# The first four panels of the output projection, each one head output earlier

## The reference, cut to what matters

```python
gla_o = merge_heads(rms_norm(gla_o, gla_norm_w[layer]))        # 4 heads of 256
hgrn_o = merge_heads(rms_norm(hgrn_o, hgrn_norm_w[layer]))     # 4 heads of 128
xo = merge_heads(rms_norm(xo, xattn_norm_w[layer]))            # 4 heads of 128
mixed = jnp.concatenate([gla_o, hgrn_o, xo], axis=-1).astype(dtype)
mixed = mixed * jax.nn.silu(gate)                              # 256 x 2048
x = x + jnp.einsum('bse,ed->bsd', mixed, w_out[layer]).astype(dtype)   # w_out 2048 x 1024
```

## Time and profile before

| what | us |
|---|---|
| median of 3 runs (lowest, highest) | 1028.63 (1028.36, 1029.28) |
| the profiled execution, its own time | 1030.11 |
| span of the profiled execution, first to last instruction | 1028.3 |
| TensorE busy | 1004.7 |
| VectorE, ScalarE, GpSimd busy | 534.0, 486.5, 765.5 |

### The profile page before, as it was taken

How to read it: one execution, slowest core, us unless ns; L and a number is a source line. 1 busy time by engine, 2 the same in 40 slices (tenths; PEclk the granted TensorE clock), 3 DMA queues, 4 the chain that set the end, 5 groups by cost and what they waited for, 6 DMA issues and landing times.

```text
span 1028.3 us, 21621 instructions
## 1 busy us (share of the span) xinstructions
PE 1004.7 (98%) x8212; PEld 984.2 (96%) x8212; DVE 534.0 (52%) x898; ACT 486.5 (47%) x748; POOL 765.5 (74%) x602
## 2 busy tenths in 40 slices
PE   9999999999999999999999899999999989999996
PEld 7999999999999999999899899999999989999996
DVE  5925984457544444504755463466656464444203
ACT  6543324456654444444566534433255554444441
POOL 2896666657999888996586845577539929999993
PEclk9999999999999999999999899999999999999998
DMA  9563334343565555555462213433226726665561
GB/s 319 163 203 127 123 105 143 119 128 107 181 198 183 175 171 174 165 174 181 126 186 91 72 54 114 142 125 122 85 65 199 215 95 195 195 196 184 173 185 58
DMA packets 48330, 154.62 MB, mean 150 GB/s; under 512 B 6060, under 2 KB 11188, under 8 KB 48264
## 3 DMA queue, kind: packets, MB, share of 16 engines
q1 hardware_dynamic: 46112, 151.31, 47.3%
q10 hardware_dynamic: 2152, 2.38, 0.7%
HBM read 151.57 MB, written 2.10 MB: 149 GB/s over the span
## 4 chain that ended last, share of the span: by engine, by line
PE 88%; DVE 4%; ACT 3%; POOL 2%; issue 1%; DMA 1%; SPq 0%; DVEq 0%; ACTq 0%
PE panel L1659 69%; PE panel L1709 3%; PE aux L1812 2%; POOL wlo L622 2%; PE panel L1759 1%; DMA memk<-in_mem_panels 1%; PE aux L2058 1%; PE aux L2069 1%; PE panel L1745 1%; PE aux L2032 1%; DVE tmp L1080 1%; PE aux L2098 1%; PE aux L2107 1%; PE aux L2021 1%; PE aux L1929 1%
## 5 line engine op out<-in xcount | busy, mean ns | idle before, releaser
L622 POOL TENSOR_TENSOR wlo<-raw,whi 128x512 fp32r<-128x512 f32 x554 | 736.4, 1358 | 239.7 <-ACT whi L722 221.3
L1659 PE MATMUL panel<-xh,whi 128*128 128x256 f32 (+1 forms) x1440 | 417.9, 290 | 4.7 <-DVE xl L1069 4.1
L1659 PE MATMUL panel<-xh,wlo 128*128 128x256 f32 (+1 forms) x1440 | 411.1, 285 | 0.0
L1659 PE MATMUL panel<-xl,whi 128*128 128x256 f32 (+1 forms) x1440 | 410.4, 285 | 0.0
L722 ACT ACTIVATE whi<-raw 128x1024 fp32r<-128x1024 f32 x280 | 293.9, 1053 | 217.7 <-PE panel L1659 184.3
L1659 PEld LDWEIGHTS panel<-xh,whi 128*128 128x128 f32 x1440 | 273.7, 190 | 7.3 <-issue 4.2
L1659 PEld LDWEIGHTS panel<-xh,wlo 128*128 128x128 f32 x1440 | 273.5, 190 | 0.0
L1659 PEld LDWEIGHTS panel<-xl,whi 128*128 128x128 f32 x1440 | 272.9, 190 | 0.2
L1659 PE MATMUL panel<-hh,wlo 128*128 128x272 f32 (+1 forms) x352 | 100.4, 285 | 0.0
L1659 PE MATMUL panel<-hh,whi 128*128 128x272 f32 (+1 forms) x352 | 100.1, 284 | 0.0
L1659 PE MATMUL panel<-hl,whi 128*128 128x272 f32 (+1 forms) x352 | 99.9, 284 | 0.0
(11 more groups left out here) (328 smaller groups left out, 1580.4 us busy)
## 6 DMA issues: line engine op xcount, KB each, us to landing
raw<-in_panels SPq DMA_DIRECT2D x232, 512.0 KB, 3.6
raw<-in_down SPq DMA_DIRECT2D x32, 448.0 KB, 3.2
raw<-in_down SPq DMA_DIRECT2D x16, 512.0 KB, 3.4
memk<-in_mem_panels SPq DMA_DIRECT2D x4, 512.0 KB, 7.9
memx<-in_mem SPq DMA_DIRECT2D x4, 256.0 KB, 5.7
h<-in_x SPq DMA_DIRECT2D x1, 1024.0 KB, 8.7
spill<-h ACTq DMA_DIRECT2D x1, 1024.0 KB, 4.6
h<-spill ACTq DMA_DIRECT2D x1, 1024.0 KB, 7.2
```

The lines of the kernel that those rows point to most:

```text
L622: ins = nc.gpsimd.tensor_tensor(wlo[:, slot, half], raw[:, slot, half], whi[:, slot, half].bitcast(f32), ALU.subtract)
L1659: ins = M(bank[:, 0:w], wt[:, slot, P * t:P * t + P], x[:, kk, c0:c0 + w], start=first and m == 0 and n == 0, stop=last and m == len(pairs ...
```

## The change

The step `("wout", k)` stands at q = k + 5 instead of q = k + 6, for k = 0 to 3. All else, and the order within one q, stays.

```diff
         steps += [("o", q)] if q < 8 else []
         steps += [("o_norm", q - 1)] if 1 <= q < 9 else []
         steps += [("o_split", q - 2)] if q >= 2 else []
-        steps += [("wout", q - 6)] if q >= 6 else []
+        steps += [("wout", q - 5)] if 5 <= q < 9 else []
     return steps
```

## The result

| | before | after |
|---|---|---|
| median us (lowest, highest), 6 runs each | 1028.95 (1028.36, 1030.85) | 1033.91 (1032.49, 1034.48) |
| span of the profiled execution | 1028.3 | 1032.7 |
| its own time | 1030.11 | 1034.48 |

The ratio is 1.0044, 95% interval 1.0032 to 1.0056. The time forecast was 1032.6 (1030.2 to 1034.8). The changed kernel was timed twice more beside other kernels, with ratios 1.0042 (1.0029 to 1.0055) and 1.0041 (1.0027 to 1.0055).

The account below looks back on a forecast made before the run. TensorE, busy 98% of the span, was taken to bound the kernel. Losses of 1.27 us (front) and 2.67 us (tail) gave 3.94 us on 1028.63: 1032.6 us, range 1030.2 to 1034.8.

Parts of the forecast that it names:

- What bounds the stretch: Head outputs into output projection and feed-forward: TensorE, busy 98% of the span; time it loses there stays missing.
- Rival (c): Feed-forward: the loss is given back later because something other than TensorE sets the time; 1028.6 us, chance 0.04.
- The front: Panel 0, now right after unit 4's column sums, waits after 18 matmuls for unit 3's low part; loss 1.27 us.
- Rival (d): Panel 0 and tail: faster, panel 0 covers TensorE's waits and unit 3 and the tail come in time; 1027.9, chance 0.03.
- The tail: Panel 4, one panel less of cover after unit 7's column sums: TensorE waits for unit 6's low part; loss 2.67 us.
- Rival (b): Tail: only the front loses, as VectorE gets through without GpSimd; 1029.9 us, chance 0.12.
- unbroken chain: From 286.68 us, 1536 matmuls without a break; expected still unbroken to the first feed-forward's end, shifted by 3.9 us.
- rival (a): Panel 4's new wait: the clock falls to half, costing 1.5 to 1.7 us more; 1034.2 us, chance 0.26.
- if the granted clock falls near 250 us: Sign, at panel 4's new wait, that the prediction is wrong.
- the forecast's case: Front and tail waits both cost time, without a clock fall; 3.94 us slower, 1032.6 us, chance 0.45.
- The sum: Whole kernel: 1.27 of the front plus 2.67 of the tail, 3.94 us on 1028.63.

Follow-up runs that it names:

- e8: Changed kernel with 32 idle matmuls on TensorE ahead of its wait for the low part of unit 6; ratio 1.0090 against the kernel before.
- e1: Kernel before with only panel 0 moved ahead of unit 6, panels 1 to 3 where they were; ratio 1.0012 against the kernel before.
- e3: Changed kernel with GpSimd waiting for the low part of unit 7 before making panel 6's low part; ratio 1.0020 against the kernel before.
- e2: Kernel before with panel 2 directly behind panel 1, ahead of the column sums of unit 7; ratio 1.0021 against the kernel before.
- The third profile: The changed kernel itself, unedited, run again beside the kernel with 9 idle matmuls; 1032.64 us, ratio 1.0041 against the kernel before.
- the second: The changed kernel itself, unedited, profiled again beside other kernels; 1036.22 us, ratio 1.0042 against the kernel before.

## Why the prediction was right, step by step

- **What bounds the stretch.** Right. The marker moved by 4.13 and the span by 4.4; e8 added 4.6 more to the marker, and 4.7 by the ratios arrived in the time. Rival (c) falls.
- **The front.** Forecast: wait after 18 matmuls, panel 0 over at 232.69, the sums of unit 5 at 235.28, loss 1.27. Measured: wait 1.73, 232.57 and 235.16, in an execution 0.08 us earlier: loss 1.23. The removed 0.49 us is gone as said. e1 shows the wait by itself. Rival (d) needed the low part of unit 3 by 229.95; it ended at 231.54.
- **The tail.** Forecast: from the sums of unit 7 to the low part of unit 6 as before, 6.57 us, with GpSimd in the same place. Measured: 244.26 to 250.79, 6.53, GpSimd at 244.11 and 247.27 as forecast (244.4 and 247.5). The wait was 2.37 (forecast about 2.3), and unit 7 was not waited for. That GpSimd makes up most of it was an argument from a few rows; e3 shows it: 2.1 of the 2.37. Rival (b) falls. That the old length came back so closely rests on GpSimd standing in the same place, counted from the end of the column sums of unit 7, to 0.1 us; in e2, with another place of it, the same cut in cover cost 2.19.
- **The rest.** From the sums of unit 7 to the marker the changed kernel took 46.47 us, before 46.37 with a panel of 2.84 more in it: 2.94 against the 2.67 forecast. The missing 0.27 is mostly a third wait that I did not see: two steps from one matmul to the next, at 285.85, took 0.55 us where others take 0.25. So the "unbroken chain" of the forecast is broken once. In the first panel of the feed-forward TensorE waits for the last low part of its input, at 286.13 in the chain above. The operation that makes it ran longer:

```profile
280.85 1.16 DVE L1304 SCALAR_TENSOR_TENSOR xl<-h,vec,xh 128x256 fp32r<-128x256 f32 x1 [0.65 <-ACT xh L865]
```

```profile
284.59 1.53 DVE L1304 SCALAR_TENSOR_TENSOR xl<-h,vec,xh 128x256 fp32r<-128x256 f32 x1 [0.65 <-ACT xh L865]
```

The first row is of the kernel before, the second of the changed one: 1.53 us instead of 1.16, in the place where GpSimd is busy throughout. The third profile has the same break (row of 1.50); the second, where the row took 0.96, has none. That the shift moved this row against GpSimd's is likely, but no run tests it. I had taken all behind panel 4 as unchanged because no row showed TensorE waiting there; the slack was not looked up.
- **The clock, rival (a).** It was given 0.26 and a price of 1.5 to 1.7. One of three profiles of the changed kernel has it, at 1.50 us. So the sign of being wrong "if the granted clock falls near 250 us" came up once in three, and the forecast's case twice. The likeliest case had no clock fall, so the rival would add to a mean and not to the forecast; how often it comes is open.
- **The sum.** 3.94 forecast; 4.13 in the marker, 4.2 to 4.5 by the three ratios, 3.1 to 5.0 by the medians. The median of 1033.91 is 1.3 above the forecast of 1032.6: 0.2 is the marker, 0.3 the kernel before, which came out at 1028.95 instead of 1028.63, and the rest (0.8) lies within the spread of the executions, which no term of the sum covers.

## What to carry to other kernels

When a block of TensorE work is moved forward in a hand-written order, it leaves a hole where it stood: list every chain that it covered there (here from the column sums of unit 7 to the low part of unit 6, which stands behind unit 7's gate) and compare lengths, not only the wait that it is meant to fill. A chain's length in a trace is not its arithmetic: see which of its rows run longer than their median, which neighbour stands beside them, and whether that neighbour will stand there again. And a new wait on TensorE can cost more than its length: here 1.5 us on top of 2.37, in one profile of three.

## What was not expected of the hardware

- The clock fell at the end of a wait of 2.37 us with dense work on both sides, in one profile of three with this wait; full speed came back between 254 and 255 us. Behind the wait of 2.58 us near 827 us it fell in all 13 profiles, behind the front wait of 1.69 to 1.73 us in none of the seven that have it. The Trainium skill ("TensorE: Matmul & The Clock Gate", section "HAM oscillation — how this bites in real kernels") tells of clocks falling in waits between bursts of matmuls, with longer waits than this. Here 2.37 us was enough once, and the fall cost 1.50 us.
- A plain fp32 matmul of 128 columns took 0.223 us (7.14 for 32, in 64 rows of e8), longer than one of 256 columns on rounded operands at 0.118.
- A panel of the same 24 matmuls takes 2.82 or 2.85 us in different stretches at full granted clock, in e3 twice 2.95. No run explains it.
